# A two-layer decoder step: the FFN's down projections moved behind its gate and up projections and done as block products

## The reference

```python
h = _rmsnorm(x, P['norm_ffn_g'][layer]) * (1 + mod[:, 4]) + mod[:, 3]
gu = h @ P['ffn_w_gate_up'][layer]
x = x + mod[:, 5] * ((jax.nn.silu(gu[..., :FFN_HIDDEN]) * gu[..., FFN_HIDDEN:]) @ P['ffn_w_down'][layer])
```

## Time and profile before

| | |
|---|---|
| median of the 3 runs | 2408.56 us |
| the runs | 2410.48, 2408.56, 2407.17 us |
| span of the profiled execution | 2404.5 us |
| PE busy | 2353.1 us (98%) |
| DVE busy | 1270.1 us (53%) |
| ACT busy | 720.9 us (30%) |
| POOL busy | 784.4 us (33%) |
| mean DMA rate | 104 GB/s |

### The profile page before, as it was taken

How to read it: one execution, slowest core, us unless ns; L and a number is a source line. 1 busy time by engine, 2 the same in 40 slices (tenths; PEclk the granted TensorE clock), 3 DMA queues, 4 the chain that set the end, 5 groups by cost and what they waited for, 6 DMA issues and landing times.

```text
span 2404.5 us, 40632 instructions
## 1 busy us (share of the span) xinstructions
PE 2353.1 (98%) x17143; PEld 2241.9 (93%) x17143; DVE 1270.1 (53%) x2529; ACT 720.9 (30%) x1154; POOL 784.4 (33%) x652
## 2 busy tenths in 40 slices
PE   7999999999999999999999999999999999999998
PEld 5997888678999999999999999988999999999998
DVE  5367743567645555544556321546655555444556
ACT  5122234426322222222224311144522222222224
POOL 3221111213344443343333342122443334443441
PEclk9999999999999999999999999999999999999999
DMA  9424343861222122222222688311111111111111
GB/s 307 169 69 134 113 147 104 300 232 36 71 88 88 54 88 71 79 80 89 88 71 71 219 275 299 125 37 36 36 53 53 37 52 46 43 53 54 53 54 73
DMA packets 163985, 249.35 MB, mean 104 GB/s; under 512 B 6164, under 2 KB 150825, under 8 KB 162526
## 3 DMA queue, kind: packets, MB, share of 16 engines
q1 hardware_dynamic: 150762, 179.29, 22.8%
q0 software_dynamic: 4784, 63.31, 7.6%
q10 hardware_dynamic: 8260, 4.15, 0.6%
HBM read 228.04 MB, written 62.54 MB: 121 GB/s over the span
## 4 chain that ended last, share of the span: by engine, by line
PE 77%; DVE 1%; ACT 1%; POOL 0%; issue 0%; ACTq 0%; DVEq 0%
PE ps L2909 33%; PE ps L2938 11%; PE ps L2939 11%; PE ps L2940 11%; PE ps L3100 4%; PE ps L3054 3%; PE ps L3235 1%; PE ps L3123 1%; PE ps L3427 0%; POOL w_slot L2708 0%; PE ps L3270 0%; DVE x L1924 0%; PE ps L3144 0%; PE ps L3137 0%; DVE tmp L2498 0%
## 5 line engine op out<-in xcount | busy, mean ns | idle before, releaser
L2909 PE MATMUL ps<-h_hi,w_slot 128*128 128x352 f32 x2112 | 538.8, 329 | 2.9 <-DVE acc_s L2015 1.4
L2699 POOL TENSOR_TENSOR w_slot<-w_raw,w_slot 128x512 fp32r<-128x512 f32 x240 | 315.2, 1345 | 581.8 <-DVE w_sum L2082 543.3
L2909 PE MATMUL ps<-f_hi,w_slot 128*128 128x352 f32 x1920 | 467.4, 323 | 0.0
L2014 DVE SCALAR_TENSOR_TENSOR x<-ps,mod,x 128x704 f32<-128x704 f32 (+1 forms) x384 | 270.5, 746 | 287.8 <-PE ps L2909 287.5
L2909 PEld LDWEIGHTS ps<-h_hi,w_slot 128*128 128x128 f32 x2112 | 371.7, 189 | 21.8 <-issue 18.7
L2938 PE MATMUL ps<-h_hi,w_slot 128*128 128x264 f32 x1280 | 364.8, 285 | 0.0
L2939 PE MATMUL ps<-h_lo,w_slot 128*128 128x264 f32 x1280 | 364.1, 284 | 0.0
L2940 PE MATMUL ps<-h_hi,w_slot 128*128 128x264 f32 x1280 | 362.8, 283 | 0.0
L2909 PE MATMUL ps<-h_lo,w_slot 128*128 128x352 f32 x1056 | 340.2, 322 | 0.0
L2909 PEld LDWEIGHTS ps<-f_hi,w_slot 128*128 128x128 f32 x1920 | 334.0, 188 | 4.1 <-issue 4.1
L2685 POOL TENSOR_TENSOR w_slot<-w_raw,w_slot 128x512 fp32r<-128x512 f32 x132 | 176.1, 1361 | 481.6 <-ACT w_slot L1432 472.8
(11 more groups left out here) (397 smaller groups left out, 3524.7 us busy)
## 6 DMA issues: line engine op xcount, KB each, us to landing
w_raw<-in_ada_w SPq DMA_DIRECT2D x48, 1024.0 KB, 5.4
w_raw<-in_ffn_w_gate_up SPq DMA_DIRECT2D x44, 1024.0 KB, 5.1
out_kv_sample<-in_cache_b_kv POOLq DMA_DIRECT2D x8, 4088.0 KB, 21.5
w_raw<-in_ffn_w_down SPq DMA_DIRECT2D x22, 1024.0 KB, 4.9
w_raw<-in_e_w_in SPq DMA_DIRECT2D x11, 1024.0 KB, 5.5
w_raw<-in_o_w_in SPq DMA_DIRECT2D x10, 1024.0 KB, 17.3
cache<-in_cache_b_kv SPq DMA_DIRECT2D x16, 512.0 KB, 6.5
out_kv_sample<-in_cache_b_kv POOLq DMA_DIRECT2D x8, 1016.0 KB, 8.7
```

What stands on the lines that cost most here:

```text
L2014: dve.scalar_tensor_tensor(dst, src, g, dst, ALU.mult, ALU.add)
L2699: pool.tensor_tensor(w_slot[slot_of(it.raw)][:, c], w_raw[it.raw.slot][:, c], w_slot[it.hi[0]].bitcast(F32)[:, c], ALU.subtract).then_inc( ...
L2909: mm = pe.matmul(big(t)[:, b, 0:BLK], wt, xt[:, k, b * BLK:b * BLK + BLK], start=(k == 0 and n == 0), stop=(k == K - 1 and n == 2))
```

## The change

The FFN becomes two parts.

Part one makes gate and up of all units, gate and up directly behind each other, with no down projection between them. Of the hidden values of units 0 to 8 DVE makes four block sums (`hidden_sums`), ACT their high part and DVE their low part; SP stores three straight blocks and four sums, high and low, to DRAM (`f_out`, `store_hidden`). The values of unit 9 are stored plain. Hidden values alternate between two buffers, the second of which (`tmp_x`) lies where `x` lies: `x` is stored to DRAM before (`x_out`, POOL) and brought back at unit 10 (`x_in`, SP). The adas of layer 0 are put between the products, three per unit up to unit 4 and two up to unit 8, and all load into one buffer in the place of `x`.

Part two does the down projection of unit 10 as before (the `filler`), then units 0 to 8 as block products, in five chunks of 1, 2, 2, 2 and 2 units (`CHUNKS`). POOL issues the loads of a chunk's operands. A chunk is four pieces, each for 256 outputs; a piece has two steps (r = 1, 0) of seven products, which are summed over the chunk's units in PSUM. Weight blocks are summed and split per piece (`words_summed`, `words_hi`, `words_lo`). DVE takes the results out (`piece_leaves`). Unit 9's down projection is done with the norm.

```diff
+CHUNKS = ((0,), (1, 2), (3, 4), (5, 6), (7, 8))
@@ def ffn(layer)
         items.append(Item("t_rest", layer=layer))
+        items.append(Item("x_out", layer=layer, n=as_made))
...
         for g in range(1, GROUPS):
...
             items.append(Item("products", of=gate, which=0))
-            split(down)
+            if g <= 8:
+                next_ada()
+            if g - 1 <= SUMMED:
+                items.append(Item("f_sums", layer=layer, j=g - 1))
+            split(up)
+            if g - 1 <= SUMMED:
+                items.append(Item("f_lows", layer=layer, j=g - 1))
+            items.append(Item("f_out", layer=layer, j=g - 1))
+            if g == GROUPS - 1:
+                items.append(Item("x_in", layer=layer))
             items.append(Item("products", of=gate, which=1))
-            for m in range(4):
-                items.append(Item("down_tile", of=down, m=m))
...
+            if g <= 8:
+                next_ada()
             sums_split(up)
             items.append(Item("products", of=up, which=0))
+            if g <= 4:
+                next_ada()
...
+            items.append(Item("products", of=up, which=1))
+        ada_out()
+        items.append(Item("piece_load", of=made[1]))
+        items.append(Item("f_load", layer=layer, chunk=0))
+        items.append(Item("f_load", layer=layer, chunk=1))
+        for m in range(KT):
+            items.append(Item("down_tile", of=filler, m=m))
+            if m == 2:
+                items.append(Item("piece_words", of=made[0]))
+        items.append(Item("piece_load", of=made[2]))
+        items.append(Item("f_last", layer=layer))
+        for piece in made:
...
+            if p + 1 < PIECES:
+                items.append(Item("piece_words", of=made[p + 1]))
...
+            if piece.m == 0 and 0 < piece.chunk < len(CHUNKS) - 1:
+                items.append(Item("f_load", layer=layer, chunk=piece.chunk + 1))
+            items.append(piece)
@@ ACT
             def copy_gate_p1(it, r):
-                act.wait_ge(hid_lo, ...)
-                copy_p1(it, tmp, r)
+                if r and it.j == 1:
+                    act.wait_ge(x_stored, 16 * (it.layer + 2))
...
+                copy_p1(it, hidden_of(it), r)
@@ SP, item "ada"
+                    if it.k == 28:
+                        sp.wait_ge(x_stored, 32)
@@ POOL
+                elif it.kind == "x_out":
+                    pool.wait_ge(xs_added, it.n)
...
+                    pool.dma_start(d_xf[it.layer], x.rearrange("p k n -> p (k n)")).then_inc(x_stored, 16)
@@ DVE
+            def piece_leaves(it):
...
+                for i, r in enumerate(PAIRS):
...
+                    done(P1_LEFT)
+                    if it.chunk:
+                        dve.tensor_tensor(u, one_, u, ALU.add).then_inc(piece_left, 1)
+                    else:
+                        dve.tensor_copy(u, one_).then_inc(piece_left, 1)
+                    done(P5_LEFT)
+                    add_to_x(m1, B1[r], two, g1).then_inc(piece_left, 1)
+                    done(P7_LEFT)
+                    made(P5_LEFT)
+                    add_to_x(m1, B1[r], three_, g1).then_inc(piece_left, 1)
+                    done(P6_LEFT)
+                    dve.tensor_tensor(u, four, u, ALU.add).then_inc(piece_left, 1)
+                    done(C11_LEFT)
+                    add_to_x(m0, B0[r], one_, g0).then_inc(piece_left, 1)
+                    done(C12_LEFT)
+                    add_to_x(m0, B1[r], two, g0).then_inc(piece_left, 1)
+                    done(C21_LEFT)
+                    add_to_x(m1, B0[r], three_, g1).then_inc(piece_left, 1)
+                    if it.chunk == len(CHUNKS) - 1:
+                        made(C21_LEFT)
+                        add_to_x(m0, B1[r], u, g0)
+                        add_to_x(m1, B1[r], u, g1)
+                        add_to_x(m1, B0[r], u, g1).then_inc(u_added, 1)
@@ PE
+            def piece_products(it):
...
+                def product(step, r, chain, weights, o, start=True):
+
+                    for u in range(U):
+                        high, low = weights(u)
+                        x_hi, x_lo = [operand(it.chunk, u, half, o, HALF[r]) for half in range(2)]
+                        for n, (w, xt) in enumerate(((high, x_hi), (high, x_lo), (low, x_hi))):
+                            mm = pe.matmul(ps[:, chain_bank(step, chain), 0:QB], w, xt, ...)
...
+                    product(step, r, 3, summed(1), T2)
+                    pe.wait_ge(piece_left, 7 * step + P1_LEFT)
+                    product(step, r, 0, straight(1, 0), B21, start=False)
```

More of the change, by code:

```diff
@@ L167 @@
     sums_hi: object = None
+    chunk: int = 0
+    units: tuple = ()
+    words: object = None
+    word_sums: object = None
+    loaded: int = 0
 @dataclass(eq=False)
@@ L560, in ffn, with next_ada @@
         items.append(Item("t_rest", layer=layer))
+        items.append(Item("x_out", layer=layer, n=as_made))
+        filler = Item("f_down", weights="ffn_w_down", col=FIRST_DOWN, layer=layer, gate=5, j=FIRST_DOWN, big=take("big", 8))
+        made = [Item("piece", layer=layer, k=4 * c + m, m=m, chunk=c, units=CHUNKS[c], gate=5, n=take("piece"))
+                for c in range(len(CHUNKS)) for m in range(4)]
+        def next_ada():
+            ada_out()
+            if layer == 0 and len(ada_units) < ADA_UNITS:
+                ada_units.append(Item("ada", k=len(ada_units), misc=take("misc")))
+                ada_open.append(ada_units[-1])
+                items.append(ada_units[-1])
         for g in range(1, GROUPS):
-            down = Item("f_down", weights="ffn_w_down", col=g - 1, layer=layer, gate=5, j=g - 1, big=take("big", 8))
             up = seven("f_up", layer, g)
@@ L1234, in o_stores @@
         def o_stores(step):
[L1236 removed]
+            return 16 + 16 * sum(2 if n >= 32 else 1 for n in range(step + 1) if o_slot(n) == o_slot(step))
         def o_before(step):
```

537 lines of the change are left out of this document (403 added, 134 removed).

## The result

The changed kernel takes **2549.9 us** (median of 4 runs, 2542.3 to 2552.7) against 2409.0 us for the kernel before (4 runs): ratio 1.0583, 95% interval 1.0564 to 1.0602. It is slower, as forecast, but by 141 us instead of 23; the range of 2402 to 2464 missed it. The profiled execution spans 2549.0 us, 144.5 more than before. A second timing of the same kernel on another chip gave 2547.3 us (2544.8 to 2555.3, ratio 1.0592).

What follows compares the result with a forecast made beforehand. The prediction took PE, busy 98% of 2404.5 us, as the bound. Its terms, from -44.6 us for matmuls removed, summed to +23.3 us, giving 2427.8 us, and with 4.1 us from span to median 2432 us; range 2402 to 2464.

Steps and rivals of the forecast that it cites:

- matmuls removed: Down projections of nine units per layer: 168 matmuls of 264 columns replace 144 of 352, -44.6 us.
- wait for x, with its clock: Unit 1's gate: ACT's first copy waits until x is stored, +26.9 us; PE's lower clock behind it, +3.4 us.
- ACT's order: Ups with no ada ahead: ACT's copy comes 0.4 us late behind the weight sums' high part, +5 us.
- adas: Layer 0, units 1 to 8: the second ada's load, queued behind f_out, lands 1.3 us late, +10 us.
- DVE in the gates: Each gate: DVE's hidden sums, weight sums and low part fit by under 1 us, costed at nothing.
- chunk 0 and before it: Part two's start: DVE bounds chunk 0, and PE waits for the last hidden values before the filler, +18.2 us.
- last chunk: Part two's last chunk: three more DVE additions per step, +2.2 us per layer, +4.4 us in all.
- part two, DMA: Part two: loads of the chunks' operands are covered by the time of the chunks, costed at nothing.
- a sign of being wrong: Layer 1: a unit of gate and up above 42.5 us would show the forecast wrong.
- rival B: Part two: chunks are bound by DMA and come late, 26 us per layer, 2484 us; chance 0.13.
- Rival C: Part two's products: matmul spacing does not hold, 159 ns each, 113 us more, 2545 us; chance 0.03.

Runs made afterwards that it cites:

- e3: The changed kernel with the store of x put ahead of POOL's low parts of unit 1's gate weights: 2529.1 us, ratio 1.0510.
- e14: e10 with layer 0's low parts of the hidden sums right behind the sums on DVE: 2430.5 us, ratio 1.0101.
- e9: The changed kernel with the hidden block sums ahead of a unit's first ada instead of behind it: 2532.3 us, ratio 1.0518.
- e4: The changed kernel with the hidden sums' low parts and the stores behind the gate's second half and second ada: 2534.9 us, ratio 1.0537.
- e2: The changed kernel with chunks 2 to 4 loaded in four parts, one at each piece of the chunk before: 2518.8 us, ratio 1.0471.
- e8: The changed kernel with six sevenths of the bytes of chunks 3 and 4 not loaded, chunk 2's load whole: 2501.7 us, ratio 1.0403.
- e10: The changed kernel with e3, e9, e4's order in layer 1 alone, and chunk loads in parts at the first (two), second and third piece: 2439.9 us.
- e11: The changed kernel with DVE making the next piece's word sums between the takes of a piece's two halves: 2526.7 us, ratio 1.0502.
- e15: e14 with ACT instead of DVE making the copy of the first product in chunk 0: 2437.2 us, ratio 1.0129.
- e17: e14 with the next piece's word sums behind a piece's first take on DVE, in chunk 0 alone: 2431.5 us, ratio 1.0111.
- e1: The changed kernel with a gap behind each operand in DRAM, so chunk rows are 2112 bytes instead of 14784: 2566.1 us, ratio 1.0667.

## Why the prediction was wrong

The sign was right, and so was the kind of most steps. Two waits priced at nothing, 31.7 and 64 us, made up most of the 118 us by which the forecast was short. By its own steps, both layers together (the measured column is of the profiled executions, 144.5 us apart; the last row is what is left of them):

| step | predicted us | measured us |
|---|---|---|
| matmuls removed | -44.6 | -44.6 |
| wait for x, with its clock | 26.9 + 3.4 | 19.9 + 4.6; e3: 21 |
| ACT's order | 5 | 2.8 (12 waits of 0.23) |
| adas | 10 | 11.0 (8.2 in a second profile) |
| DVE in the gates | 0 | 31.7 |
| chunk 0 and before it | 18.2 | 25 |
| last chunk | 4.4 | 12 |
| part two, DMA | 0 | 64 |
| clock behind the other waits, and rest | 0 | 18 |

**Matmuls removed.** Right. In e14, where no wait is left in them, chunks 1 to 3 take 122.9 and 123.0 us, against 3 x 4 pieces x 84 matmuls x 0.1215 = 122.5. In the changed kernel itself the term can't be read off alone: from unit 1's gate to the last down projection it takes 744.5 and 699.7 us where the kernel before took 663.9 and 637.5, that is 142.8 more, and with 44.6 us of matmuls fewer the waits and the slower clock there must be 187.4 us.

**The wait for x.** Right in place and chain, a quarter too dear at 26.9 for 19.9: I took the 16.6 us of the earlier trace rows; the two transfers land 13.0 and 14.0 us after issue. The issue in layer 0 came 2 us later than I had it (621.33 for 619.3), but so did the gate (622.25 for 620.42), so that this cost nothing. The sentence on the Trainium skill's price (DMA: Bandwidth & Descriptors, "Anatomy of one DMA") said 11.9 us for a transfer, an estimate, and 17.5 us for the two waits; the trace, with 13.0 and 14.0 and with 19.9, is nearer to it than to mine.

**DVE in the gates: the first failed step.** The text had "It fits, by under 1 us, so I cost it at nothing", with the price of a misfit at "up to 1 us" on each of 18 gates. It fell on 18 gates, at 1.8 us each, and a unit of layer 1 took 42.8 us, above the 42.5 that the prediction had given as a sign of being wrong. Two things were missed: in layer 1 DVE's weight sums now run beside POOL's low parts (1.6 us more, the rows of the gate), and in layer 0 the hidden sums queue behind the ada's addition. e9 shows the second by taking it away (19.4 to 3.1 us). e4 shows that what DVE does ahead of the first combination is what makes both late; that POOL is what stretches it in layer 1 rests on the durations alone. The Trainium skill (SBUF — State Buffer, "SBUF: two separate sides") says that an instruction of VectorE with two inputs in SBUF and one of GpSimd that reads SBUF exclude one another for its whole length. The trace agrees as far as durations tell, 0.69 at most alone and up to 1.79 beside POOL; no run here took POOL's work away alone.

**Part two, DMA: the step that failed most.** "Covered, at nothing" compared the bytes of a chunk with the time of a chunk, and that holds: PE waits for a chunk's operands in no run but e2. It left out who else uses the DMA engines, namely the next piece's words, issued 2 us behind 7.57 MB, and what stands behind those on DVE. Price: six waits of 8.8 to 9.2 us, 53.6 together, and with the clock and the shorter waits 64 us in chunks 1 to 3 (154.5 and 155.0 us for 122.5). e2, e8, e10 and e11 remove these waits by other handles: fewer bytes ahead, and DVE not standing there (e8 four of the six, by its design). The prediction's rival B had the same resource, with the chunks themselves late, which did not happen; that its 52 us are near the 64 is luck.

The Trainium skill (DMA: Bandwidth & Descriptors, "Queues, rings and completion order") says that each DMA engine takes turns between the queues it has work for, a packet at a time. The trace agrees: 352 packets of POOL's queue against 347 of SP's in 12 us, and 456 against 466 in e1. Fair turns are no fair share of bytes, since each 1,024 bytes of the words wait for 14,784 of the chunk. In the trace a packet of the chunk takes 576 ns in the mean and one of the words 47. Of the chunk's 512 packets 138 had gone before the words' first, at 2315.6 us; the other 374 turns on 16 engines are 14.6 us, an estimate, which ends at 2330.2. The 512th packet of the words starts at 2330.1 us, and the chunk's last at 2330.8.

**Chunk 0.** The mechanism is right for the later pieces: DVE is full there (97%), and neither order nor another engine helps much (e15 to e17). The size was 7 us short: 30.6 and 32.1 us for 28.5, and 3.1 us before it for 1.8. The first words land after 9.3 and 10.8 us (PE idle 1.7 and 3.2), with a granted clock of 0.78 in the piece behind them in layer 1.

**Last chunk.** Mis-sized: 46.9 us in both layers for 40.8, 6 a layer and not 2.2. It is the same in e14 (47.0 and 46.9), so no late words are in it. The stretch in layer 0 (stretch, length, busy PE, PEld, DVE, ACT, POOL; clock, DMA share, GB/s):

```profile
1319.90:1366.90 47.00, 42.84 (x340) 41.56 (x339) 43.06 (x110) 8.60 (x8) 19.52 (x10) 1.00 0.20 68
```

DVE's work is 10.8 us a piece and not the 10.1 that I had added up, so that it is above PE's 10.2 and not below it. That DVE sets the pace is argued from this; no run took the three additions away.

**The clock.** Granted clock of PE in part one, layer 0, of the change, and of e14 in the same stretch (stretch, length, busy, clock, DMA share, GB/s):

```profile
622.00:1075.00 453.00, 412.84 (x3435) 0.97 0.53 178
```

```profile
622.00:1075.00 453.00, 442.07 (x3725) 0.99 0.54 185
```

Before, it was 1.00 there. I had priced the clock behind the long wait only. But from 640 to 1075 us, where it is over and no wait of PE is longer than 2.9 us, the clock still reads 0.98, and 1.00 before the change: the small waits lower it too. 0.976 over the whole span for 0.992 is up to 40 us of slower clock, a part of it while PE was idle anyway.

Rival C's time, 2545 us, is close by accident: it said that the spacing of matmuls fails, and in e14's chunks 1 to 3 it is 122 ns for the 121.5 of before.

## What to carry to other kernels

When a small load is issued behind a large one on another queue, do not price it by its bytes. Compare the packets: here both queues had 512, so the small load took as long as the large one still needed. Then look what stands behind it in the queue of the engine that reads it: there the late load becomes idle time of others. "It fits by under 1 us" is a price and not a zero in a stage where VectorE and GpSimd read SBUF side by side, or where a wait for another engine's work stands in the same queue. An account of bytes per stage says only that the stage's own loads are in time, not what they delay. And moving a store means asking for every reader that waits for it.

## What the runs showed of the hardware

- Between two queues the DMA engines moved packets one for one, whatever their size: 352 of 14,784 bytes against 347 of 1,024 in 12 us of the changed kernel, 456 of 4,224 against 466 of 1,024 in 6 us of e1 (both counts with the few of 4 bytes that end a load).
- The second 256 KB load of a piece's words landed 19.5 to 19.9 us after its issue when 7.57 MB in rows of 14,784 bytes had been issued just ahead of it, 9.5 to 11.0 us behind 3.79 MB (e10), 4.9 to 6.9 us behind 1.89 MB (e2, e10), and after 3.0 us with nothing ahead.
- With rows of 2112 bytes POOL needs 1.0 us to issue a 1848 KB load instead of 0.55, and in ten of ten places of e1 the third load of a series is issued 0.34 to 0.36 us after the second has landed, 10.9 to 13.5 us late; with rows of 14,784 bytes four are issued one behind the other. Why was not tried.
- DVE's additions of two SBUF inputs, 512 columns, take 0.69 us at most alone (138 in the changed kernel) and have a median of 1.49 us, up to 1.79, where they overlap an instruction of POOL (22).
